# Gate blocks taken three at a time, VectorE in the norm scaling, and later squares in a two-layer encoder trunk

## The reference, cut to what matters

```python
# layer 0, mixer: convolution module; layer 1, mixer: windowed attention
h = modulate(rms_norm(x, norm_mix[i]), sh1, sc1)
x = x + g1 * mixer(h)                    # last product: w_pw2 (layer 0), w_o (layer 1)
h = modulate(rms_norm(x, norm_ffn[i]), sh2, sc2)
g, u = split(h @ w_gu[i])                # 2048 -> 2 x 5632
x = x + g2 * ((silu(g) * u) @ w_down[i]) # 5632 -> 2048
# after both layers
y = rms_norm(x, norm_out)
# rms_norm(x, g) = x * rsqrt(mean(x*x over channels) + eps) * g
# modulate(h, shift, scale) = h * (1 + scale) + shift, shift and scale per batch item
```

## Time and profile before

| | us |
|---|---|
| median of 3 runs | 3349.31 (3344.06 to 3625.43) |
| profiled execution, its own time | 3347.12 |
| its span on the slowest core (core 2) | 3346.0 |
| PE busy | 3041.8 (91%) |
| DVE busy, ACT busy, POOL busy | 1221.0, 752.7, 335.1 |
| mean granted PE clock, core 2 | 0.959 |
| spans of the other seven cores | 3325.3 to 3341.2 |

### The profile page before, as it was taken

One profiled execution on the slowest core, in us unless ns is written; L12 is line 12 of the kernel. 1 busy time (PEld: TensorE's weight loads), 2 busy tenths in 40 slices (PEclk: granted clock), 3 DMA queues, 4 the chain that ended last, 5 costly groups with the idle time before them and its releaser, 6 DMA issues.

```text
span 3346.0 us, 58403 instructions; the slowest of 8 cores (3325.3 to 3346.0 us)
## 1 busy us (share of the span) xinstructions
PE 3041.8 (91%) x23532; PEld 1857.9 (56%) x23566; DVE 1221.0 (36%) x2690; ACT 752.7 (22%) x1743; POOL 335.1 (10%) x510
## 2 busy tenths in 40 slices
PE   2399996889999999999999889898999999999996
PEld 0155553455556565565565555455566666666653
DVE  0356677331321414123413548723131313132315
ACT  1412224571000000000002647646100000000012
POOL 0000005000000000000001035410000000000000
PEclk8599997999999999999999999799999999999998
DMA  9977774525757475674667123032674444343432
GB/s 218 150 113 126 128 127 90 118 51 101 127 99 133 75 134 104 110 130 76 109 126 120 23 55 58 18 70 51 115 127 75 76 73 79 64 80 54 84 61 104
DMA packets 73592, 320.57 MB, mean 96 GB/s; under 512 B 11952, under 2 KB 28176, under 8 KB 45808
## 3 DMA queue, kind: packets, MB, share of 16 engines
q0 software_dynamic: 49440, 283.78, 48.9%
q1 hardware_dynamic: 23888, 33.06, 3.3%
HBM read 590.55 MB, written 10.70 MB: 180 GB/s over the span
## 4 chain that ended last, share of the span: by engine, by line
PE 81%; DVE 5%; ACT 5%; DMA 4%; issue 3%; another core or an unknown queue 1%; SPq 0%; DVEq 0%; ACTq 0%; POOL 0%; POOLq 0%
PE ps L229 80%; ACT SCR L232 2%; DMA RING<-wmod 2%; ACT HBraw L232 1%; DMA X<-xT 1%; PE ps L1349 1%; DVE X L933 1%; DMA RING<-wpw 1%; ACT RING L232 1%; DVE X L465 1%; DVE UBraw L578 1%; DVE UBraw L1355 1%; DVE X L456 0%; SPq L224 0%
## 5 line engine op out<-in xcount | busy, mean ns | idle before, releaser
L229 PE MATMUL ps<-HBraw,RING 128*128 128x384 bf16 (+4 forms) x10816 | 1762.4, 325 | 35.8 <-DVE HBraw L562 15.0
L229 PEld LDWEIGHTS ps<-HBraw,RING 128*128 128x128 bf16 x10848 | 1050.2, 98 | 716.1 <-issue 56.3
L229 PE MATMUL ps<-UBraw,RING 128*128 128x384 bf16 (+3 forms) x6016 | 968.9, 319 | 41.6 <-ACT SCR L232 22.1
L229 PEld LDWEIGHTS ps<-UBraw,RING 128*128 128x128 bf16 x6016 | 571.4, 99 | 403.9 <-issue 78.7
L620 DVE TENSOR_TENSOR UBraw<-ps,SCR 128x384 bf16<-128x384 f32 (+2 forms) x264 | 144.4, 547 | 1194.7 <-PE ps L229 1175.7
L232 ACT ACTIVATE SCR<-ps 128x384 f32<-128x384 f32 (+2 forms) x264 | 127.0, 481 | 1787.2 <-PE ps L229 1787.2
L465 DVE SCALAR_TENSOR_TENSOR X<-ps,MOD,X 128x384 f32<-128x384 f32 (+2 forms) x960 | 389.6, 447 | 319.9 <-PE ps L229 318.7
L224 POOL DMA_DIRECT2D RING<-wgu x88 | 46.5, 529 | 1094.6 <-PE ps L229 1091.1
L229 PE MATMUL ps<-SCT,RING 128*128 128x3 bf16 x3072 | 91.3, 165 | 64.3 <-DMA RING<-wmod 54.4
L224 POOL DMA_DIRECT2D RING<-wmod x96 | 51.5, 537 | 877.5 <-PE ps L229 869.1
L229 PEld LDWEIGHTS ps<-SCT,RING 128*128 128x128 bf16 x3072 | 89.8, 97 | 74.9 <-issue 66.8
(11 more groups left out here) (95 smaller groups left out, 1235.3 us busy)
## 6 DMA issues: line engine op xcount, KB each, us to landing
RING<-wmod POOLq DMA_DIRECT2D x96, 1024.0 KB, 13.6
RING<-wgu POOLq DMA_DIRECT2D x88, 1024.0 KB, 8.9
RING<-wdn POOLq DMA_DIRECT2D x80, 512.0 KB, 8.2
RING<-wpw POOLq DMA_DIRECT2D x24, 1024.0 KB, 17.0
X<-xT SPq DMA_DIRECT2D x4, 2368.0 KB, 55.6
RING<-wqkv POOLq DMA_DIRECT2D x16, 512.0 KB, 6.5
X<-xT SPq DMA_DIRECT2D x32, 192.0 KB, 2.4
RING<-wo POOLq DMA_DIRECT2D x5, 1024.0 KB, 8.5
```

Of the source, the lines that this page charges most:

```text
L229: return PE.emit(nc.tensor.matmul(out, lhsT=lhsT, rhs=rhs, start=start, stop=stop, **kw))
```

## The change

1. `ffn` takes gate blocks 0, 1 and 2 tile by tile (before: 0 and 1); after the first gate group all adds in `late` are written. The small modulation blocks that were streamed from gate block 2 on come from block 3 on.
2. `factors` puts `samples` ahead of tile 2's rows in `behind` (before: behind them).
3. In `scale`, every third channel row (c % 3 == 2, 5 of 16) gets its second pass on DVE, the others on ACT as before.
4. The add of a square is due 3 groups later (before 2). In `wo_group` the square itself is also written one group later, ahead of the next group's epilogue.
5. PE's wait for `q_6` and `q_7` moves from ahead of the first K group to the first Q group that reads them.
6. In FFN 1's last down group, block 0 goes over all tiles first, then seven blocks in tile order 2, 1, 0 (before: eight blocks in tile order 0, 1, 2).

```diff
-                j = 2 + (m - 40) * 6 // 8
+                j = 3 + (m - 40) * 5 // 8
...
-                late.append((pe_groups[0] + 2, lambda: self.add(t, i, ta)))
+                late.append((pe_groups[0] + 3, lambda: self.add(t, i, ta)))
...
                 if self.out:
+                    if t == 2:
+                        behind.append((1.5, t, lambda: self.samples(tr)))
                     for c in range(KC):
                         behind.append((0.62, t, lambda c=c: self.scale(t, c, tr)))
-                    if t == 2:
-                        behind.append((1.5, t, lambda: self.samples(tr)))
...
-                ACT.wait(DVE.tick())
-                act(HB[:, c, 32 + xlo:32 + xlo + zn], self.tmp[:, i, 0:zn], AF.Identity, scale=AM[:, c, 0:1],
-                    bias=MOD[:, self.li, self.sh0 + c, 0:1])
-                self.tfree[i] = ACT.tick()
+                am, sh, row = AM[:, c, 0:1], MOD[:, self.li, self.sh0 + c, 0:1], HB[:, c, 32 + xlo:32 + xlo + zn]
+                if c % 3 == 2:
+                    DVE.wait(DVE.tick())
+                    DVE.emit(nc.vector.tensor_scalar(out=row, in0=self.tmp[:, i, 0:zn], scalar1=am, scalar2=sh,
+                                                     op0=ALU.mult, op1=ALU.add))
+                    self.tfree[i] = DVE.tick()
+                else:
+                    ACT.wait(DVE.tick())
+                    act(row, self.tmp[:, i, 0:zn], AF.Identity, scale=am, bias=sh)
+                    self.tfree[i] = ACT.tick()
...
-        def tile_outer(blocks, tiles, body):
-            for t in range(3):
+        def tile_outer(blocks, body, order=(0, 1, 2)):
+            for t in order:
...
-                    two = [ring_use(f"gu{li}_{j}") for j in js[:2]]
+                    some = {}
                     for t in range(3):
-                        for j in (0, 1):
-                            gate_up(two[j][0], j, t, G)
+                        for j in js[:3]:
+                            if t == 0:
+                                some[j] = ring_use(f"gu{li}_{j}")
+                            gate_up(some[j][0], j, t, G)
+                            if t == 0 and j == js[0]:
+                                flush_late()
                             if t == 2:
-                                ring_release(two[j][1])
-                    js = js[2:]
+                                ring_release(some[j][1])
+                    js = js[3:]
...
-                inner = 5 if after.out else 0
+                inner = 5 if after.out else 1
...
-                tile_outer([ring_use(f"dn{li}_{G}_{b}") + (2 * b,) for b in range(inner, 8)], tiles,
-                           lambda slot, n, t: down(slot, n, t, G))
+                tile_outer([ring_use(f"dn{li}_{G}_{b}") + (2 * b,) for b in range(inner, 8)],
+                           lambda slot, n, t: down(slot, n, t, G), (0, 1, 2) if after.out else (2, 1, 0))
...
-        q3 = [use_halves("q_6"), use_halves("q_7")]
+        q3 = []
...
             for n in range(12, 16):
+                if t == 0 and n % 2 == 0:
+                    q3.append(use_halves(f"q_{n // 2}"))
...
-            norm3.square(n, t, epilogue_bias(1, n, xlo, zn, bk, PE.tick()))
+            if last:
+                norm3.square(*last.popleft())
+            last.append((n, t, epilogue_bias(1, n, xlo, zn, bk, PE.tick())))
```

More of the change, by code:

```diff
@@ L590, in tile_outer @@
                         body(slot, n, t)
-                    if t == 2:
+                    if t == order[2]:
                         ring_release(bi)
@@ L996, in build_nc @@
             ring_release(bi)
-        tile_outer([ring_use(f"pw2_{b}") + (2 * b,) for b in (5, 6, 7)], L0T, pw2_group)
+        tile_outer([ring_use(f"pw2_{b}") + (2 * b,) for b in (5, 6, 7)], pw2_group)
         norm2 = Norm(UBraw, L0T, 1, 0)
@@ L1444, in build_nc @@
         pk = 0
+        last = deque()
         def wo_group(rows, n, t):
@@ L1470, in build_nc @@
                 ring_release(i)
-        tile_outer([ring_use(f"wo_{b}") + (2 * b,) for b in (5, 6, 7)], L1T,
+        tile_outer([ring_use(f"wo_{b}") + (2 * b,) for b in (5, 6, 7)],
                    lambda slot, n, t: wo_group(whole(slot), n, t))
+        norm3.square(*last.popleft())
         DVE.wait(kv_t[0], kv_t[1])
```

## The result

The changed kernel took **3309.4 us** in its profiled execution, against 3347.1 for the kernel before, and its time is 0.9896 of that before, 95% interval [0.985, 0.9943]. Run again beside the last experiments it gave 0.9888 [0.9871, 0.9904]. So it is faster by 1.0 to 1.1%, less than the 2% that the prediction took as what a measurement tells from no change. The prediction was 3301 with a range of 3283 to 3319. In some executions, whichever kernel ran, the cores of one die were granted a lower clock; these are in no time, median or ratio here, though they set the raw medians of the first comparison (3539.9 after, 3487.4 before).

The account below looks back on a forecast made before the run. It took PE's chain to be four fifths matmuls, so only PE's idle time and clock could move. Terms 5 + 11 + 6 + 24.5 - 1 = 45.5 us off 3347.1 gave 3301 us, 80% range 3283 to 3319.

Parts of the forecast that it names:

- A: Stretch where `pw2` goes over into FFN 0, with 16.0 us of PE idle; gain of 5 us claimed.
- C: Stretch from `wo` into FFN 1, with 21.7 us of PE idle; gain of 6 us claimed.
- B: Stretch from FFN 0's last down group into K and V, 13.3 us of PE idle; gain of 11 us claimed.
- D: FFN 1's last down group and the tail after it; gain of 24.5 us claimed.
- small: One more place per layer where two modulation blocks touch; 1 us lost.
- new wait ahead of the second gate group: Start of each FFN: PE waits for Ln behind SiLU and two table loads, 7 us, then some 13 in FFN 1.
- wait for `q`: First K group: PE's 3.11 us wait and 1.7 us of clock go, as the block is first read 14 us later.
- K bank's: K and V stage: PE's 2.0 us wait for the K bank stays at 1.5 us.
- tail: After PE's end in FFN 1's last down group, to the span's end: 16.8 us instead of 18.5.
- cover: FFN weight ring: gate block 3 already loaded behind the three held blocks, giving 16 us before later loads are needed.
- rival of late weights: From gate block 3 on, weight loads come late, 24 blocks losing 139 us; 3440 us, chance 0.03.
- A and C give nothing: FFN starts: ACT falls behind a little more, leaving four long waits and their clock; 3313 us, chance 0.22.

Follow-up runs that it names:

- Experiment 8: Changed kernel with all late adds written right after each FFN's first gate group's matmuls, ahead of its SiLU; 3297.1 us.
- experiment 3: Changed kernel with each FFN's second gate group in PSUM banks 4 and 5 instead of 2 and 3; 3304.5 us.
- experiment 5: Changed kernel with the square in `wo` written at once behind its own epilogue, adds still 3 groups late; 3305.1 us.
- experiment 4: Changed kernel with adds due 2 groups after their square, as before the change, instead of 3; 3329.0 us.
- Experiment 1: Changed kernel with two gate blocks tile by tile instead of three, and modulation blocks at their old places; 3307.4 us.
- experiment 2: Changed kernel with modulation blocks at gate blocks 3, 3, 4, 5, 5, 6, 7, 7, so no two pairs at neighbouring gate blocks; 3306.5 us.
- experiment 9: Changed kernel with modulation blocks spread as in experiment 2 and each pair split around a gate group; median 3292.2 us, 0.9837 of the time before.
- five edits: Changed kernel with the edits of experiments 8, 2, 5 and 3 and the split of experiment 9; 3275.1 us profiled, 0.9789 of the time before.

## Why the prediction was right, and where it failed

By the prediction's own steps; measured values are the table's:

| step | forecast | measured |
|---|---|---|
| A | 5 | 6.7 in pw2, -0.6 in the front: 6.1 |
| C | 6 | 12.4 in wo, -6.0 in the front: 6.4 |
| B | 11 | 13.1, less 2.1 in the K and V stage: 11.0 |
| D | 24.5 | 23.8 |
| small | -1 | bodies: -4.1 and -6.4 |
| sum | 45.5 | 37.7 in device time (38.4 from pw2 to end) |

**A and C: right in mechanism, and in size partly by luck.** The new wait ahead of the second gate group was forecast as 7 and some 13 us, with tables loaded twice; it is 6.6, and 9.6 behind two of about 3.2 between the last adds, 15.9 in all. The clock's 3 us behind it is 2.7. The sums came out because two misses cancel: the forecast had 4 us from `pw2` and 9 from `wo`, and these gave 6.7 and 12.4, while the fronts lost 1.6 and 3.0 more than forecast. Experiment 8 takes most of the wait away in both layers, experiment 3 in A. The price was taken for the table loads as the earlier trace rows shows them, 1.28 us with the next activation right behind; the trace after has both loads so (734.51 to 735.80, 736.31 to 737.61). The Trainium skill (ScalarE: Activation LUTs, What ACT_TABLE_LOAD costs) adds a drain of 1.38 per switch; no run here shows one in this running queue. The forecast also said that the held square puts ACT behind by 6.4 us at the end of `wo`; experiment 5 is in line with this, with 6.5 us less of waiting in the front of FFN 1. What it did not say is that the held square and the later add are two ways to the same delay, so that one of them was enough for `wo`: 95.0 without the held square, 99.1 with it and the add of before. That the held square would have given the first 8 us alone, with adds due after 2 groups, is argued from experiment 4; no run had all else as before.

**B and D: right in the sum.** The wait for `q` went, the K bank's stayed (1.83 against 1.5 forecast). But B's 11 was made up otherwise: of it the forecast gave 4.8 to the wait for `q` and its clock, and experiment 4 leaves 1.9 when the add is early again (B 2.7 shorter than before, K and V 0.8 longer), so the later add brought 9.1. In the place of the wait for `q` PE now waits for rows of `HB` in the first K group (1.8 us), which the forecast did not have. In D, PE's part was forecast as 71.3 and took 75.1, and the tail as 16.8 and took 14.3. The tail before was also misread: 3327.5 is the end of PE's last product group, while its last add ends at 3329.5, so PE was unused for 16.5 us, not 18.5. D starts at once, the first factors cost 3.29 (2.9 forecast). The forecast that tile 0's groups would be paced by DVE without waits was off in form, not in sum: there are four waits of 0.9 to 1.7 us.

**Small: wrong, the step that failed.** The prediction said "behind them block 3 already lies in the ring, 16 us of cover" and charged one pair of modulation blocks with 1 us in both layers together. What the runs showed is three costs of a pair of 1 MB loads and their blocks. (1) The cover was as forecast, 17.5 us, but the load behind a pair is the third of three in the queue and lands after 20.9 us, not 13.6, so that cover is not enough: 2.9 us a core. (2) The clock falls behind a pair, and for longer where a wait for weights follows (6.8 us at half speed on core 0, else 3.4): lengthened groups went from 2.5 to 7.4 us a core (the clock in all of the bodies from 4.3 to 9.2), where the prediction charged clock only behind the long waits of the fronts. (3) Each further pair waits 0.6 for its first half, as forecast: 1.5 over both FFNs on core 0. Together 9.3 of the 10.5 lost. Experiment 1 shows that both of the first two come with the third block and the moved places, together; experiment 2 takes away most of (1) by the places alone, and experiment 9 all of (2). The rival of late weights had the mechanism of (1), but its price (3440) supposed a wait at every block.

The rival "A and C give nothing" gave a closer time (3313) than the forecast, for a reason that was not the case.

## What to carry to other kernels

When work is reordered, list for every queue which loads are now issued together, and price the last of them by the load of that place in a burst, not by the median. Small matmuls that wait for each other are best laid singly between long groups: here that was worth 14 us (experiment 9 against 2), while a whole third tile-by-tile block brought 1. And before an order of adds and activations is tuned by counts, look at which function each engine has to switch to in between: one call moved ahead of a SiLU gave 12 us.

## What the runs showed of the hardware that was not expected

- PE's clock fell after pauses far shorter than those of the earlier trace rows: behind two 3-column blocks of 0.95 us with 0.6 us of waiting between them, the next 96 matmuls took 17.87 instead of 16.19 us (or 16.15 instead of 14.48) at some of the places, and at others not. With each 3-column block between gate groups of 5.8 us or more, none of the 8 cores of experiment 9 had a fall of the clock in the FFN bodies, and the 8 cores with five edits, whose pairs are apart as well, had six, each at a wait of 1.4 to 2.1 us for gate weights; a wait of 1.84 us in experiment 9 had none.
- Three 1 MB loads issued within 3 us took 11.1, 16.0 and 20.9 us, with the DMA engines busy to 0.80 in the window that follows: about 5 us more for each place in the burst. The next three took 11.4, 15.7 and 21.1.
- The second pass of a row on DVE (384 columns, f32 to bf16) took 0.48 us, where 0.42 had been taken between the earlier trace rows. It did not matter.

```profile
L548 DVE TENSOR_SCALAR HBraw<-SCR,AM,MOD 128x384 bf16<-128x384 f32 x25 | 12.0, 480 | 2.7
```
